# Strassen's scheme for the gate and up products of a hybrid layer, with weight sums kept in DRAM and the feed-forward in three groups of tiles

## The reference

```python
h = _rmsnorm(x, norm_mix[0])
mix, hg_s = _hgrn2(h, 0, hg_s, hg_w_in, hg_lower_bounds, hg_out_gain, hg_w_out)
x = x + mix
gate, up = jnp.split(_rmsnorm(x, norm_ffn[0]) @ ffn_w_gu[0], 2, axis=-1)
x = x + (jax.nn.silu(gate) * up) @ ffn_w_down[0]
```

## Time and profile before

| | |
|---|---|
| runs, median | 2713.87 us (2713.65 to 2716.33, 3 runs) |
| profiled execution, span | 2714.6 us, 0.7 us above the median |
| around the span | the page gives no other time of this execution; sums are made against the span |
| TensorE busy | 2683.8 us |
| VectorE, ScalarE, GpSimd busy | 1417.0, 1125.0, 382.3 us |
| transfers | 258.08 MB, mean 95 GB/s |
| block 0 | output stage until about 352 us, gate and up until 633.5, down until 775 |
| blocks 1 to 3 | about 644 us each; in block 1 down begins at 1294 and ends at 1418 |

### The profile page before, as it was taken

One profiled execution on the slowest core, in us unless ns is written; L12 is line 12 of the kernel. 1 busy time (PEld: TensorE's weight loads), 2 busy tenths in 40 slices (PEclk: granted clock), 3 DMA queues, 4 the chain that ended last, 5 costly groups with the idle time before them and its releaser, 6 DMA issues.

```text
span 2714.6 us, 46083 instructions
## 1 busy us (share of the span) xinstructions
PE 2683.8 (99%) x14692; PEld 2341.6 (86%) x14692; DVE 1417.0 (52%) x2376; ACT 1125.0 (41%) x1963; POOL 382.3 (14%) x285
## 2 busy tenths in 40 slices
PE   8999999999999999999999999999999999999998
PEld 7999999999988887888878887888888888788887
DVE  6666643443346765444436666444444676544443
ACT  5555432222245554333335555433324555433332
POOL 3111111110011112111011111111101111211101
PEclk9999999999999999999999999999999999999999
DMA  5322322223332223333342222333343222333334
GB/s 183 94 59 61 102 78 85 81 81 98 122 110 67 80 66 93 95 94 99 114 143 83 74 73 78 93 97 97 100 133 119 70 78 66 93 97 93 100 113 139
DMA packets 136837, 258.08 MB, mean 95 GB/s; under 512 B 15776, under 2 KB 15808, under 8 KB 136528
## 3 DMA queue, kind: packets, MB, share of 16 engines
q1 hardware_dynamic: 136368, 248.59, 30.9%
q0 software_dynamic: 384, 8.44, 0.9%
HBM read 245.16 MB, written 18.14 MB: 97 GB/s over the span
## 4 chain that ended last, share of the span: by engine, by line
PE 96%; DVE 1%; issue 1%; ACT 1%; POOL 0%; DMA 0%; ACTq 0%; SPq 0%; POOLq 0%; DVEq 0%
PE ps L362 29%; PE ps L364 29%; PE ps L363 29%; PE ps_u L272 1%; PE ps_s L251 1%; PE ps_o L285 1%; PE ps_u L273 1%; PE ps_o L287 1%; PE ps_o L286 1%; PE ps_k L262 1%; PE ps_u L236 0%; DVE h_lo L708 0%; PE ps_s L298 0%; PE ps_s L299 0%; DMA xres<-x_t 0%
## 5 line engine op out<-in xcount | busy, mean ns | idle before, releaser
L362 PE MATMUL ps<-h_hi,w_hi 128*128 128x512 f32 (+1 forms) x3040 | 1091.8, 359 | 12.4 <-DVE h_lo L708 10.1
L703 DVE TENSOR_TENSOR w_lo<-w_raw,w_hi 128x512 fp32r<-128x512 f32 x864 | 670.5, 781 | 805.4 <-ACT w_hi L603 803.3
L364 PE MATMUL ps<-h_hi,w_lo 128*128 128x512 f32 (+1 forms) x3040 | 1071.8, 353 | 0.0
L363 PE MATMUL ps<-h_lo,w_hi 128*128 128x512 f32 (+1 forms) x3040 | 1070.9, 352 | 0.0
L603 ACT ACTIVATE w_hi<-w_raw 128x512 fp32r<-128x512 f32 x864 | 538.0, 627 | 680.7 <-PE ps L364 480.9
L362 PEld LDWEIGHTS ps<-h_hi,w_hi 128*128 128x128 f32 x3040 | 572.2, 188 | 87.5 <-issue 9.0
L364 PEld LDWEIGHTS ps<-h_hi,w_lo 128*128 128x128 f32 x3040 | 572.6, 188 | 73.4
L363 PEld LDWEIGHTS ps<-h_lo,w_hi 128*128 128x128 f32 x3040 | 572.9, 188 | 69.0 <-issue 1.4
L362 PE MATMUL ps<-a_hi,w_hi 128*128 128x512 f32 (+1 forms) x1200 | 431.4, 359 | 3.5 <-DVE w_lo L703 2.2
L364 PE MATMUL ps<-a_hi,w_lo 128*128 128x512 f32 (+1 forms) x1200 | 429.1, 358 | 0.0
L363 PE MATMUL ps<-a_lo,w_hi 128*128 128x512 f32 (+1 forms) x1200 | 428.7, 357 | 0.0
(11 more groups left out here) (128 smaller groups left out, 1989.5 us busy)
## 6 DMA issues: line engine op xcount, KB each, us to landing
w_raw<-w_all SPq DMA_DIRECT2D x868, 256.0 KB, 2.6
xres<-x_t SPq DMA_DIRECT2D x32, 256.0 KB, 2.8
y_t<-fbuf SPq DMA_DIRECT2D x24, 256.0 KB, 2.9
xres<-x_t SPq DMA_DIRECT2D x8, 288.0 KB, 5.4
y_t<-fbuf SPq DMA_DIRECT2D x8, 288.0 KB, 3.1
ret_zero<-zeros POOLq DMA_DIRECT2D x1, 2048.0 KB, 7.5
state_smp<-state_in SPq DMA_DIRECT2D x1, 512.0 KB, 5.6
state_s<-state_smp SPq DMA_DIRECT2D x1, 512.0 KB, 3.5
```

Of the source, the lines that this page charges most:

```text
L362: pe.matmul(o, w_hi[:, ring, kk, :], hh, start=(k == 0), stop=False)
L363: pe.matmul(o, w_hi[:, ring, kk, :], hl, start=False, stop=False)
L364: last_mm[0] = pe.matmul(o, w_lo[:, ring, kk, :], hh, start=False, stop=stop)
L703: nc.vector.tensor_tensor(w_lo[:, r, :, :], w_raw[:, r, :, :], w_hi[:, r, :, :].bitcast(F32), ALU.subtract).then_inc(w_lo_ready, 1)
```

## The change

Weights and data of gate and up are taken as 2 x 2 blocks: rows of the weight pair are (gate, up), its columns and the rows of the data are the two halves of D (4 tiles of 128 each), and columns of the data are the two halves of the block's frames. The Winograd form of Strassen's scheme needs 7 products of such blocks instead of 8. For tile j the weight operands are A11, A12, A22 as they come, and the sums S1 = A21 + A22, S2 = S1 - A11, S3 = A11 - A21, S4 = A12 - S2; the data operands are B11, B21, B22 and T1 to T4. Each product is 4 x 3 matmuls of T/2 columns.

- **Data sums.** In the output stage VectorE scales each tile of `xres` by the norm's gain into `h2_raw`, makes T1 to T4, and high and low parts of 7 operands are kept in `h2`. The output tiles come in the order TILE_AT, so that the halves of D meet. `norm_ffn` no longer goes through `residual_tile`.
- **Weight sums.** In block 0 GpSimd makes S1 to S4 for each j. ScalarE and VectorE split 7 operands of 4 tiles per j (before: 4 pieces). SP stores S3, S4 and both parts of S1 and S2 to DRAM (6 x 256 KB per j). In blocks 1 to 3 SP loads 9 x 256 KB per j: A11, A22, A12, S3, S4 (split again, ALONE) and both parts of S2 and S1 (PAIRED).
- **Additions after the products.** P1 + U2 and so on are made by ScalarE (2 copies) and VectorE (4 additions, one over two banks) per j. `xrstd` is no longer multiplied in for the up half: it is applied to the down product.
- **Groups.** The feed-forward goes in groups of 8, 8 and 6 tiles. Each group's down product is 8 tiles of 2 pieces; VectorE multiplies by `xrstd` (`dn_done`) and adds `xres` (`acc_done`), into `xres`, in the last group into `fbuf`. The loads of the next block's input stand behind `acc_done` of the last group.
- **Queue order.** `load_pair(b, 0)` stands ahead of piece 6 of the output projection in SP's program and waits for the last `y_lo`.

```diff
-GU0 = OUT0 + KT * P_OUT
-DN0 = GU0 + FT * P_GU
+DN0 = OUT0 + KT * P_OUT
+GROUPS = ((0, 8), (8, 8), (16, 6))
+P_GROUP = 2 * KT
+TILE_AT = (0, 4, 1, 5, 2, 6, 3, 7)
+A11, S2, A22, S1, S3, A12, S4 = range(OPERANDS)
+PAIRED = (S2, S1)
+ALONE = (A11, A22, S3, A12, S4)
...
+    bank_of = (bank_a, bank_b, bank_e, bank_d, bank_c, bank_a, bank_d)
+    def split_of(b):
+        return tuple(range(OPERANDS)) if first(b) else ALONE
...
@@ TensorE
+            def bank_free(J, o):
+                if o == A11:
+                    wait(pe, g_copied, 2 * J)
...
+                elif o == A12:
+                    pe.wait_ge(g_copied, 2 * J + 1)
+                elif o == S4:
+                    pe.wait_ge(g_added, 4 * J + 3)
+            def strassen(b, T, o, k0, k1):
+                n = T // 2
+                out, part = bank_of[o][:, 0:n], H_OF[o]
+                more = o in (A12, S4)
+                for k in range(k0, k1):
...
+                    pe.matmul(out, g_hi[:, o, k, :].bitcast(F32R), hh, start=(k == 0 and not more), stop=False, skip_group_check=True)
+                    pe.matmul(out, g_hi[:, o, k, :].bitcast(F32R), hl, start=False, stop=False, skip_group_check=True)
+                    mm = pe.matmul(out, g_lo[:, o, k, :].bitcast(F32R), hh, start=False, stop=last, skip_group_check=True)
+            def down(b, T, f):
+                j0, tiles = GROUPS[f]
+                J = FT * b + j0 + tiles
+                with pe.Fori(0, KT // 2) as i:
+                    for s in range(2):
+                        pe.wait_ge(dn_done, len(GROUPS) * KT * b + KT * f + 2 * i + s + 1)
...
+                        pe.wait_ge(g_added, 4 * J)
...
@@ VectorE
             def output_tile(b, T, i, s):
...
+                nc.vector.tensor_scalar(out, two(xres[:, m, 0:T], T), gffn[:, m:m + 1], None, ALU.mult).then_inc(h2_raw_ready, 1)
+            def h2_sums(b, T, i):
...
+                nc.vector.tensor_tensor(part(T1), b12, part(B11), ALU.subtract).then_inc(h2_raw_ready, 1)
+                nc.vector.tensor_tensor(part(T3), part(B22), b12, ALU.subtract).then_inc(h2_raw_ready, 1)
...
+            def gate_up(b, T, j, j0, more, begun=True):
...
+                nc.vector.tensor_tensor(u2[:, 0:n], bank_b[:, 0:n], p1u3[:, 0:n], ALU.add).then_inc(g_added, 1)
...
+                dve.wait_ge(g_done, OPERANDS * J + S3 + 1)
+                nc.vector.tensor_tensor(p1u3[:, 0:n], bank_c[:, 0:n], u2[:, 0:n], ALU.add).then_inc(g_added, 1)
...
+                nc.vector.tensor_tensor(two(ebuf[:, 0, 0:T], T), ps[1][:, :, 0:n],
+                                        p1u3[:, None, 0:n].broadcast_to([P, 2, n]), ALU.add).then_inc(g_added, 1)
...
+                nc.vector.tensor_tensor(fbuf[:, 1, n:T], bank_d[:, 0:n], u2[:, 0:n], ALU.add).then_inc(g_added, 1)
+            def down(b, T, f):
...
+                for m in range(KT):
...
+                    if last and m > 0:
+                        residual_tile(m - 1, TB, b + 1, gmix)
+                    dve.wait_ge(pieces_done, PIECES * b + DN0 + P_GROUP * f + 2 * (m + 1))
...
+                    nc.vector.tensor_tensor(sbv(fbuf[:, s, 0:T], T), psv(s, T), sbv(xrstd[:, 0:T], T), ALU.mult).then_inc(dn_done, 1)
+                    dve.wait_ge(dn_done, no + 3)
+                    nc.vector.tensor_tensor((fbuf[:, s, 0:T] if last else xres[:, m, 0:T]), fbuf[:, s, 0:T], xres[:, m, 0:T],
+                                            ALU.add).then_inc(acc_done, 1)
...
@@ GpSimd, block 0
+            def first_sums(j):
...
+                nc.gpsimd.tensor_tensor(g_x[:, 0], g_raw[:, RAW_A21], g_raw[:, RAW_A22], ALU.add).then_inc(g_sum_ready, 1)
...
@@ SP
+            def load_kept(b, j):
...
+                if start:
+                    sp.wait_ge(y_lo_ready, HEADS * (b + 1))
...
             def block_program(b, T):
...
+                load_pieces(b, OUT0, OUT0 + RING + 2)
                 if first(b):
...
+                load_pair(b, 0)
+                load_pieces(b, OUT0 + RING + 2, DN0 + RING)
...
+                    for m in range(KT):
+                        q = DN0 + P_GROUP * f + RING + 2 * m
+                        load_pieces(b, q, q + 2)
+                        s = m % 2
+                        sp.wait_ge(acc_done, len(GROUPS) * KT * b + KT * f + m + 1)
...
                         sp.dma_start(xres[:, m, 0:TB], xsrc).then_inc(x_loaded[s], 16)
```

More of the change, by code:

```diff
@@ L419, in output_tiles, with operand_ready @@
                           OUT0 + 2 * P_OUT * i + n, n, half, KT, a_hi, a_lo)
[L421 to L434 removed]
+            def operand_ready(b, j, o):
+                if first(b) or o not in PAIRED:
+                    pe.wait_ge(g_lo_ready, split_no(b, j, o) + 1)
+                else:
+                    pe.wait_ge(g_pair_loaded[o], 32 * (FT * (b - 1) + j + 1))
@@ new lines, in down @@
+            def down(b, T, f):
[4 more added lines that the diff above has]
+                        pe.wait_ge(dn_done, len(GROUPS) * KT * b + KT * f + 2 * i + s + 1)
+                        if s == 0:
+                            pe.wait_ge(g_copied, 2 * J)
+                        pe.wait_ge(g_added, 4 * J)
+                        for half in range(2):
+                            pe.wait_ge(a_lo_ready, J - (tiles - KP if half == 0 else 0))
+                            piece(b, T, s, DN0 + P_GROUP * f + 4 * i + 2 * s + half, 2 * s + half, half, tiles, a_hi, a_lo)
@@ new lines, in gu_high @@
+            def gu_high(b, j, o):
+                J = FT * b + j
+                if o in (A11, A12, A22):
+                    act.wait_ge(g_loaded[{A11: RAW_A11, A12: RAW_A12, A22: RAW_A22}[o]], 16 * (J + 1))
+                elif first(b):
+                    act.wait_ge(g_sum_ready, 4 * j + {S1: 1, S2: 2, S3: 3, S4: 4}[o])
+                else:
+                    act.wait_ge(g_sum_loaded[o], 16 * (FT * (b - 1) + j + 1))
+                wait(act, g_done, OPERANDS * (J - 1) + o + 1)
+                if first(b) and o in PAIRED:
+                    wait(act, g_pair_stored, 64 * j)
+                nc.scalar.activation(g_hi[:, o].bitcast(F32R), operand_of(o), ACT.Copy).then_inc(g_hi_ready, 1)
@@ L880, in down @@
-            def down(b, T, i):
-                for s in range(2):
-                    m = 2 * i + s
-                    for u in range(P_DN):
-                        split_lo(b, DN0 + 2 * P_DN * i, P_DN * s + u)
-                        if u == 2 and s == 1:
-                            residual_tile(2 * i, TB, 2 * b + 2, gmix)
-                        elif u == 2 and not isinstance(i, int):
-                            residual_tile(2 * i - 1, TB, 2 * b + 2, gmix)
-                    dve.wait_ge(pieces_done, PIECES * b + DN0 + P_DN * (m + 1))
-                    wait(dve, y_stored[s], 16 * ((KT // 2) * b + i) + 1)
-                    nc.vector.tensor_tensor(sbv(fbuf[:, s, 0:T], T), psv(s, T), sbv(xres[:, m, 0:T], T), ALU.add).then_inc(y_added, 1)
+                dve.wait_ge(x1_ready, done)
@@ L918, in block_program @@
                     output_tile(b, T, 0, 1)
-                for s in range(2):
-                    residual_tile(s, T, 2 * b + 1, gffn)
+                ahead = split_of(b)
+                h2_sums(b, T, 0)
                 output_pieces(b, 1, 1 if first(b) else 2, 2 * P_OUT)
+                h2_low(b, T, 0)
+                for o in ahead[0:2]:
+                    gu_low(b, 0, o)
                 for i in range(1, KT // 2):
@@ new lines, in load_raw, with load_first @@
+            def load_raw(j, p):
+                sp.dma_start(g_raw[:, p], w_view[W_GU + P_GU * j + p]).then_inc(g_loaded[p], 16)
+            def load_first(j):
+                if isinstance(j, int) and j == 0:
+                    sp.wait_ge(y_lo_ready, HEADS)
+                    for p in range(4):
+                        load_raw(j, p)
+                    return
+                sp.wait_ge(g_sum_ready, 4 * j - 1)
+                load_raw(j, RAW_A21)
+                sp.wait_ge(g_lo_ready, OPERANDS * (j - 1) + A22 + 1)
+                load_raw(j, RAW_A22)
+                load_raw(j, RAW_A11)
+                keep(j - 1)
+                sp.wait_ge(g_lo_ready, OPERANDS * (j - 1) + A12 + 1)
+                load_raw(j, RAW_A12)
@@ L1123, in _ @@
             block_program(0, T0)
+            sp.wait_ge(g_pair_stored, 64 * FT)
+            for stored in g_sum_stored:
+                sp.wait_ge(stored, 16 * FT)
             with sp.Fori(1, BLOCKS) as b:
```

541 lines of the change are left out of this document (389 added, 152 removed).

## The result

The changed kernel takes 2916.0 us (median of 4 runs, 2913.7 to 2920.4) against 2714.7 (2713.7 to 2716.3): ratio 1.074, 95% interval 1.0727 to 1.0753. It is 201 us slower. The forecast was 2781 with a range of 2700 to 2850: the direction was right, the size was not, and the time lies 66 us outside the range. The profiled execution, whose span is 2918.7 us, is the slowest of the four.

A forecast was written before the change was run, and what follows sets the result against it. TensorE, 99% busy, was taken as the bound: number of matmuls times their spacing. Terms -88.6 + 46 + 22 + 28 + 31 + 10 + 7 + 12 = +67.4 on 2714.6 gave 2782, median 2781 us; range 2700 to 2850.

The forecast's parts named there:

- TensorE's gain: Gate and up: fewer matmuls in block 0, -35.2 us; half-width ones at 119.7 ns in blocks 1 to 3, -53.4 us.
- last group: Last feed-forward group: serial chain of 6.1 us per tile against TensorE's 4.2, +46 us, bounds 42 to 52.
- piece 6: Output projection: piece 6, issued behind nine transfers, is 7 us late three times, +22 us, bounds 15 to 30.
- output stage and its first pairs: Output stage: VectorE has 33 to 36 us of work for TensorE's 28; 7 us per block, +28 us, bounds 12 to 45.
- block 0's pairs: Block 0's gate and up: VectorE and GpSimd hold each other up at SBUF, +31 us, bounds 0 to 70.
- starts of groups: Each group's down product waits for the addition that empties bank d after S4: 0.8 us x 12, +10 us.
- S4, xrstd: Gate and up: S4 waits for p1u3 and the addition after S3, with the first pair's wait for xrstd, +7 us.
- clock: After new waits at two places per block TensorE runs at the lower clock: seven losses of 1.7 us, +12 us.
- 111 and 133: Rivals on the ns spacing of 256-column matmuls in gate and up: 111 gives 2734 us, chance 0.09; 133 gives 2856, 0.07.
- The port is held for the whole of each sum: Rival, block 0's pairs: GpSimd's sums lock the SBUF port for their full length, 70 us, total 2821; chance 0.13.
- VectorE keeps up: Rival: output stage, block 0's pairs and S4 cost nothing, the clock 2; 2706 us, faster than before; chance 0.14.
- the joints overlap more: Rival: half of 46 + 22 + 28 us at last group, piece 6 and output stage is hidden; 2734 us; chance 0.15.

The follow-up runs named there:

- both edits: Changed kernel with, in the last feed-forward group, weight pieces loaded one tile earlier and h_lo of tile m - 1 made behind the addition of tile m: 2783.8 us.
- piece 6 first: Changed kernel with SP loading pieces 6 to 9 of the output projection ahead of the transfers of gate and up's first pair: 2889.3 us.
- narrow squares: On top of piece 6 first, GpSimd's sum of squares in blocks 1 to 3 made for 16 of 512 columns: 2872.3 us.
- S4 store first: Changed kernel with SP, in block 0, storing S4 of pair j - 1 ahead of loading A22 of pair j: 2890.3 us.
- narrow sums: On top of S4 store first, GpSimd's S1 to S4 of pairs 1 to 21 made for 16 of 512 columns: 2873.1 us.

## Why the prediction was wrong

| term | forecast | measured | shown by |
|---|---|---|---|
| TensorE's gain | -88.6 | -90 | 120.0 ns in groups 2 and 3 of blocks 1 to 3, 1848 x 120.0 = 221.8 us per block; 134 ns in block 0 without waits |
| last group | +46 | +137 (111 and 26 in the heads) | both edits, -132 |
| piece 6 | +22 | +27 | piece 6 first, -27 |
| output stage and its first pairs | +28 | +40 (the rest of 66.8) and 3 x (228.5 - 221.8) = +20 | in part by narrow squares, -17 |
| block 0's pairs | +31 | +57 | S4 store first, narrow sums |
| starts of groups | +10 | +13 | the table of stretches |
| S4, xrstd | +7 | 0 in blocks 1 to 3 | in block 0 TensorE's waits do stand at S4, released by the two-bank addition (L1103); they are counted with the pairs |
| clock | +12 | inside the others | |

The measured terms sum to 204, the difference of the spans. The output stage's term is a remainder, so the sum shows that nothing is counted twice and proves no term.

**The step that failed** is "Behind each stands a chain that was hidden and still is serial: VectorE adds tile m; SP waits for acc_done and loads the next block's x into xres". The chain is right and 6.1 us long (6.43 once it stands alone), but it is not all that SP does behind this wait. In SP's program the next tile's weight pieces follow the same wait, the x load and the y store. Before, a tile had six pieces in a ring of four: its own loads and four of the next tile's stood ahead of its wait, and 15.4 us of matmuls covered the rest. With two pieces per tile the ring holds two tiles, the pieces of tile m + 3 are issued behind the addition of tile m, and the first of them must be split ahead of the addition of tile m + 1. I had followed what the wait lets through, and not what is queued behind it. The period was 9.3 us per tile and not 6.1, and the term cost 137 us and not 46. The words "No row bounds it far off: 42 to 52" kept the range narrow: the earlier trace rows show the chain of one tile with full cover, where the pieces have long landed.

**Block 0's pairs** were priced by the wrong mechanism. The mutual hold-up is there and costs 19 us of the 31 forecast. The ring through SP's queue, 28 us, was missed in the same way: I priced S1 to S4 by how long they run, and the six stores of a pair not at all, though S2 reuses S4's buffer and so waits for a store that SP issues last. Its bounds (0 to 70) did hold the result, 57, by luck: they were drawn for the hold-up alone. The sign that was to show it, VectorE near 100% at 12.5 us per pair, failed: it was busy for 38.1 of 50 us, at 13.2 per pair.

**Clock.** The seven losses of 1.7 us each failed by the number and kind of waits. In the last group TensorE waits 1.6 to 5.4 us ahead of each tile, and the granted clock is 0.88 there and 0.75 at the start of the next heads. The heads' 26 us over three blocks are two things: TensorE waits another 5.9, 3.8 and 4.6 us for the last tile's product, which is the ring, and 55 matmuls start at the lower level, some 12 us by an estimate of 0.2 us each. All of it is gone with both edits (1.00 in the two rows of that run). Over the whole kernel 511 matmuls start at the lower level, where it was 37 before; at full clock they would take some 75 us less, an estimate from their columns, of which the rings hid a part. The forecast had 12.

**The output stage** was right by the sum of VectorE's own work (33 us; 32.5 measured with narrow squares), and mis-sized: GpSimd's sums, noted for block 0 only, add 6.9 us to that work in the other blocks too. The wait was capped at 7 us per block; it was 10, and the first pair of gate and up, which needs the last data sums, waits 3.5 us more and runs some microseconds at half clock: its group takes 87.6 us, not 80.5. Differences of 0.43 us on VectorE grew to 1.5 beside the sum of squares; with what follows the hold-up is worth 17 us over the three blocks. That the rest is VectorE's load is not shown.

**Right** were the spacing of 256 columns (119.7 forecast, 120.0 measured; 111 and 133 are out), the late piece 6 (8 us, 7 forecast), the start of each group, transfers hidden in blocks 1 to 3, and that block 0's saving would be gone. Of the rivals, "The port is held for the whole of each sum" is seen in single operations, but at its price of 70 us in block 0 it is refuted (19); that VectorE keeps up and that the joints overlap more are refuted too. No rival held a second ring.
